# Eight modulation slabs as row products, fills moved to the start, chunk 3 converted early

## The reference, cut to what matters

```python
mod = silu(c) @ mod_w + mod_b                       # six vectors of 1024
sh1, sc1, g1, sh2, sc2, g2 = split(mod, 6)
h = rmsnorm(x, norm1_g) * (1 + sc1) + sh1
z = h @ w_in + b_in                                 # 1024 x 5646
x = x + g1 * mixer(z)                               # S5, mLSTM, forgetting attention, gates, w_out
h = rmsnorm(x, norm2_g) * (1 + sc2) + sh2
x = x + g2 * ((silu(h @ w1) * (h @ w3)) @ w2)       # hidden width 2816
out = rmsnorm(x, final_g)
```

## Time and profile before

| what | value |
|---|---|
| median of 3 runs | 886.14 us |
| runs | 880.66 to 889.43 us |
| the profiled execution | 881.7 us |
| its span, first to last instruction | 880.0 us |
| mean granted TensorE clock | 0.993 |
| TensorE matmul busy | 850.4 us (97%) |
| VectorE, ScalarE, GpSimd busy | 442.4, 324.9, 32.9 us |

### The profile page before, as it was taken

How to read it: one execution, slowest core, us unless ns; L and a number is a source line. 1 busy time by engine, 2 the same in 40 slices (tenths; PEclk the granted TensorE clock), 3 DMA queues, 4 the chain that set the end, 5 groups by cost and what they waited for, 6 DMA issues and landing times.

```text
span 880.0 us, 10526 instructions
## 1 busy us (share of the span) xinstructions
PE 850.4 (97%) x3936; PEld 682.3 (78%) x3936; DVE 442.4 (50%) x719; ACT 324.9 (37%) x477; POOL 32.9 (4%) x46
## 2 busy tenths in 40 slices
PE   3989999999999999999999999999999999999997
PEld 1568888877877777777888878888888888888886
DVE  4789978236779553333883373333333333322222
ACT  4454445442232443433333563333333332222221
POOL 1010000000000000000001110000000000000110
PEclk9899999999999999999999999999999999999999
DMA  8923322347884211215323323333333333333322
GB/s 302 292 68 89 89 75 74 92 153 233 283 282 150 67 53 48 67 30 167 89 80 120 95 64 99 99 97 95 95 95 95 95 95 90 90 107 90 96 77 96
DMA packets 149372, 100.67 MB, mean 114 GB/s; under 512 B 11072, under 2 KB 142552, under 8 KB 148312
## 3 DMA queue, kind: packets, MB, share of 16 engines
q1 hardware_dynamic: 146080, 100.10, 37.3%
q10 hardware_dynamic: 3256, 0.10, 0.2%
HBM read 97.03 MB, written 2.10 MB: 113 GB/s over the span
## 4 chain that ended last, share of the span: by engine, by line
PE 90%; DVE 4%; ACT 2%; issue 1%; DMA 1%; SPq 1%; POOL 0%; DVEq 0%; ACTq 0%
PE bank L1608 25%; PE bank L1610 25%; PE bank L1609 25%; PE bank L1625 2%; PE bank L1819 2%; PE bank L1749 1%; PE bank L1841 1%; PE bank L1769 1%; PE bank L1780 1%; DMA modA<-in_mod_w 1%; PE bank L1866 1%; PE bank L1832 1%; PE bank L1817 1%; DVE wlo L1115 1%; ACT whi L631 1%
## 5 line engine op out<-in xcount | busy, mean ns | idle before, releaser
L1608 PE MATMUL bank<-h_lo,whi 128*128 128x512 f32 x712 | 285.6, 401 | 4.8 <-DVE wlo L1115 2.6
L1610 PE MATMUL bank<-h_hi,wlo 128*128 128x512 f32 x712 | 278.2, 391 | 0.0
L1609 PE MATMUL bank<-h_hi,whi 128*128 128x512 f32 x712 | 277.9, 390 | 0.0
L1608 PEld LDWEIGHTS bank<-h_lo,whi 128*128 128x128 f32 x712 | 134.1, 188 | 34.7 <-issue 4.4
L1609 PEld LDWEIGHTS bank<-h_hi,whi 128*128 128x128 f32 x712 | 134.2, 189 | 28.8 <-issue 1.7
L1610 PEld LDWEIGHTS bank<-h_hi,wlo 128*128 128x128 f32 x712 | 134.1, 188 | 28.8
L1115 DVE TENSOR_TENSOR wlo<-raw,whi 128x1024 fp32r<-128x1024 f32 x61 | 74.5, 1223 | 103.3 <-ACT whi L631 103.3
L631 ACT ACTIVATE whi<-raw 128x1024 fp32r<-128x1024 f32 x61 | 64.3, 1055 | 156.4 <-PE bank L1610 115.8
L1610 PE MATMUL bank<-a_hi,wlo 128*128 128x512 f32 x176 | 68.5, 389 | 0.0
L1608 PE MATMUL bank<-a_lo,whi 128*128 128x512 f32 x176 | 68.5, 389 | 0.0
L1609 PE MATMUL bank<-a_hi,whi 128*128 128x512 f32 x176 | 68.5, 389 | 0.0
(11 more groups left out here) (326 smaller groups left out, 996.6 us busy)
## 6 DMA issues: line engine op xcount, KB each, us to landing
raw<-in_ffn_w SPq DMA_DIRECT2D x60, 512.0 KB, 3.8
raw<-in_w_in SPq DMA_DIRECT2D x44, 512.0 KB, 4.0
slab<-in_mod_w SPq DMA_DIRECT2D x32, 512.0 KB, 5.7
modA<-in_mod_w SPq DMA_DIRECT2D x4, 1024.0 KB, 11.0
modB<-in_mod_w SPq DMA_DIRECT2D x4, 1024.0 KB, 19.7
raw<-in_w_out SPq DMA_DIRECT2D x8, 512.0 KB, 3.7
raw<-in_ffn_w SPq DMA_DIRECT2D x8, 384.0 KB, 3.2
xtok<-in_x SPq DMA_DIRECT2D x4, 512.0 KB, 5.0
```

Source lines behind the costliest of these rows:

```text
L1608: mm(dst, w_h, m_l, start=first, stop=False)
L1609: mm(dst, w_h, m_h, start=False, stop=False)
L1610: return mm(dst, w_l, m_h, start=False, stop=last)
```

## The change

Five edits go together. (a) `keep_clock(12)` stands ahead of the first `mod_rows`, and `keep_clock(5)` behind the shift columns is gone. (b) `mod_rows` runs over all eight slabs, so the row copies wait for slab 7, and the eight one-column products for slab 7 are gone; each scale column is one closed product. (c) Chunk 3 gets a buffer of its own for `whi` (`whi_3`, in the place of `tab_c`, which moves to 115 KiB), and `hi(3)`, `lo(3)` stand right behind `hi(2)`, `lo(2)`. (d) The FFN starts with three chunks per tile k: ACT converts the third ahead of the `h_hi` tiles, DVE takes its `lo4` behind the first `h_lo`. (e) As that chunk fills bank 2, the 1/rms broadcast uses bank 3.

```diff
+        whi_3 = at("whi_3", [P, KB, P], F32R, 67)
-        tab_c = at("tab_c", [P, NS5, P], F32, 67)
+        tab_c = at("tab_c", [P, NS5, P], F32, 115)
...
+        def w_high(s):
+            return whi_3[:] if s == 3 else whi[:, s % 3]
...
-                if s >= 3:
+                if s >= 4:
                     act.wait_ge(w_mm, s - 2)
-                A(whi[:, s % 3], raw[:, s % 4], ACT.Copy).then_inc(w_hi, 1)
+                A(w_high(s), raw[:, s % 4], ACT.Copy).then_inc(w_hi, 1)
...
             hi(2)
+            hi(3)
             for t in range(1, S_F1):
-                if t >= 3:
+                if t >= 4:
                     hi(t)
...
+            act.wait_ge(w_loaded[(S_F1 + 2) % 4], SLOT_LOADS[S_F1 + 2])
+            A(whi4[:, (S_F1 + 2) % 4], raw[:, (S_F1 + 2) % 4], ACT.Copy).then_inc(w_hi, 1)
             for k in range(KB):
...
-            for s in range(S_F1 + 2, S_F1 + 4):
-                act.wait_ge(w_loaded[s % 4], SLOT_LOADS[s])
-                act.wait_ge(w_mm, S_F1)
-                A(whi4[:, s % 4], raw[:, s % 4], ACT.Copy).then_inc(w_hi, 1)
+            s = S_F1 + 3
+            act.wait_ge(w_loaded[s % 4], SLOT_LOADS[s])
+            act.wait_ge(w_mm, S_F1)
+            A(whi4[:, s % 4], raw[:, s % 4], ACT.Copy).then_inc(w_hi, 1)
...
             lo(2)
+            lo(3)
...
-                if t >= 3:
+                if t >= 4:
                     lo(t)
...
-                V.tensor_tensor(htmp[:, k % 4], x1g[:, k], ps[2][:], ALU.mult).then_inc(s_h2, 1)
+                V.tensor_tensor(htmp[:, k % 4], x1g[:, k], ps[3][:], ALU.mult).then_inc(s_h2, 1)
                 if k and k - 1 not in H2_POOL:
                     h2_lo(k - 1)
+                if k == 1:
+                    lo4(S_F1 + 2)
             h2_lo(KB - 1)
-            lo4(S_F1 + 2)
             lo4(S_F1 + 3)
...
-                              start=(k == 0), stop=(k == KB - 2))
-                    if k == KB - 2:
+                              start=(k == 0), stop=(k == KB - 1))
+                    if k == KB - 1:
                         ins.then_inc(s_mrow, 1)
...
-                        mm(ps[7][:, KB + 4 * n + i:KB + 4 * n + i + 1], modrow[:, n, i * P:(i + 1) * P],
-                           ones[0:1, 0:1], start=(n == 0 and i == 0), stop=False)
-                pe.wait_ge(s_mod0[KB - 1], 16)
-                for i in range(KB):
-                    ins = mm(ps[7][:, KB + i:KB + i + 1], modB[:, 3, D + i * P:D + (i + 1) * P], cf[:, KB - 1:KB],
-                             start=False, stop=(i == KB - 1))
+                        ins = mm(ps[7][:, KB + 4 * n + i:KB + 4 * n + i + 1], modrow[:, n, i * P:(i + 1) * P],
+                                 ones[0:1, 0:1], start=True, stop=True)
                 ins.then_inc(s_mod1, 1)
...
-            for k in range(KB - 1):
+            keep_clock(12)
+            for k in range(KB):
                 mod_rows(k)
...
             mod_scale_columns()
             mod_shift_columns()
-            keep_clock(5)
...
-                for w in range(2):
+                for w in range(3):
                     s = S_F1 + w
+                    if k == 0 and w == 2:
+                        pe.wait_ge(w_lo, s + 1)
                     ins = split_mm(ps[w][:], whi4[:, s % 4, k], wlo[:, s % 4, k], h_hi[:, k], h_lo[:, k],
                                    k == 0, k == KB - 1)
                     if k == KB - 1:
                         ins.then_inc(w_mm, 1)
```

More of the change, by code:

```diff
@@ L1114, in lo @@
                 dve.wait_ge(w_hi, s + 1)
-                V.tensor_tensor(wlo[:, s % 4], raw[:, s % 4], whi[:, s % 3].bitcast(F32),
+                V.tensor_tensor(wlo[:, s % 4], raw[:, s % 4], w_high(s).bitcast(F32),
                                 ALU.subtract).then_inc(w_lo, 1)
@@ L1936, in _ @@
                 for k in range(KB):
-                    ins = split_mm(ps[s % 2][:], whi[:, s % 3, k], wlo[:, s % 4, k], h_hi[:, k], h_lo[:, k],
+                    ins = split_mm(ps[s % 2][:], w_high(s)[:, k], wlo[:, s % 4, k], h_hi[:, k], h_lo[:, k],
                                    k == 0, k == KB - 1)
@@ L2009, in _ @@
             for t in range(NT):
-                ins = mm(ps[2][:, t * P:(t + 1) * P], rstd[:, t:t + 1].broadcast_to([P, P]), ident[:],
+                ins = mm(ps[3][:, t * P:(t + 1) * P], rstd[:, t:t + 1].broadcast_to([P, P]), ident[:],
                          start=True, stop=True)
@@ L2025, in _ @@
                         ins.then_inc(w_mm, 1)
[L2026 to L2032, removed]
+            s = S_F1 + 3
+            pe.wait_ge(w_lo, s + 1)
+            for k in range(KB):
+                ins = split_mm(ps[3][:], whi4[:, s % 4, k], wlo[:, s % 4, k], h_hi[:, k], h_lo[:, k],
+                               k == 0, k == KB - 1)
+            ins.then_inc(w_mm, 1)
             with pe.Fori(0, NF // 2 - 1) as i:
```

## The result

The changed kernel took 878.96 us in the median of 22 executions (876.37 to 886.08), the kernel before 886.18 us (880.02 to 889.43) beside it. The ratio is 0.9945, 95% interval 0.9925 to 0.9965: faster by 0.55% (4.9 us), clear of noise and under 1%. The sum forecast 2.2 us and 883.9; the time lies inside the range, but more was won than the sum says. Two later comparisons gave 0.9956 (0.9927 to 0.9985) and 0.9964 (0.9938 to 0.9990). All 46 executions of the changed kernel have a mean of 880.0 us, 105 of the kernel before 883.7: **3.7 us**, good to about 1 us. The 105 are those of the three later sets; with the 22 beside the first result (mean 885.3) it is 883.9, and the difference 4.0.

What follows compares the result with a forecast made beforehand. TensorE holds 90% of the chain, so only its waits, late feeding or half clock count. `modc` 1.9 us earlier plus 0.3 slack gives 2.2 us, FFN 0: from the median 886.14 to 883.9 us, range 879.0 to 888.4.

Steps and rivals of the forecast that it cites:

- Part 1: Modulation rows at the start: twelve early fills and eight slabs as rows bring `modc` 1.9 us earlier, at 39.85.
- the 0.75 us I gave them: Modulation rows: gain remaining from the early fills after ACT's copies hold the transposes, carried through slabs 4 to 7.
- Part 2: Behind the shift columns: without fills PE starts chunk 0 near 42.0; the half-clock loss lies inside the `wlo` 4 wait.
- Part 3: Chunk 3 converted early: its 2.63 us wait goes, but chunk 4 waits 1.1 to 2.8 us for `wlo` 4, starting at 69.3.
- the 0.3 of the sum: Ahead of chunk 4: slack that `wlo` 4 had, added to 1.9 us for the 2.2 us gain at the start.
- Part 4: FFN start: 0.4 us removed, 0.35 added, fifth chunk's `wlo` without cover; taken as 0.
- A: Front counts in full, `wlo` 4 no bound: 3.7 to 5.2 us by chunk 4, 880.9 us; chance 0.07.
- B: Start: clock not kept, as transposes don't count as busy, or fills late; `modc` at 41.5, 885.6 us; chance 0.25.
- C: FFN: fifth chunk's load lands late behind the new order, 0.8 us lost, 884.7 us; chance 0.13.
- D: Chunks 0 and 1 stay at half clock without fills ahead; low until 60 gives 888.1 us; chance 0.08.

Runs made afterwards that it cites:

- wlo4_first: Changed kernel with VectorE's order changed: `wlo` 4, 5 ahead of the b_blocks, `wlo` 6 ahead of the last four angle groups; ratio to before 0.9949, mean 879.0 us.
- fills_back: Changed kernel with the five fills behind the shift columns again; ratio to before 0.9974, mean 879.6 us.
- wlo4_again: Same kernel as wlo4_first, run again beside the changed kernel; ratio to before 0.9938, mean 878.1 us.
- ffn_only: Kernel before with only parts (d) and (e), three chunks per tile at the FFN start; ratio to before 1.0018, mean 885.4 us.
- wlo4_fills_back: wlo4_first's kernel with the five fills behind the shift columns again; ratio to before 0.9927, mean 878.1 us.
- start_only: Kernel before with only parts (a) and (b), the row edits and moved fills; ratio to before 0.9973, mean 881.6 us.
- chunk3_only: Kernel before with only part (c), the early conversion of chunk 3; ratio to before 0.9984, mean 882.3 us.

## Why the prediction was right, and where its sum was short

- **Part 1, `modc` 1.9 us earlier.** Measured: 2.2 in two of three traces of the changed kernel (39.54 for 41.75), set by VectorE's `wlo` 0 and 1, as written; 43.01 in the other. Over all ten traces with eight slabs as rows `modc` lies at 40.1 in the mean, over the four with the old columns at 42.05: 2.0 us. But the part of the fills in it was wrong: the 0.75 us I gave them are not there. Rows of slab 4 begin at 28.5 to 28.9 in seven of the eight traces with the fills and, without, at 28.6 or 29.2. What moved `modc` is the shift columns. They took 1.95 us in seven of ten traces with eight slabs as rows (2.03, 2.52 and 3.17 in the rest), 3.55 or more in all four with the old columns, and they ended 2.3 us sooner, though the last 512-column products ended 1.2 us later. Part of this is the order: in wlo4_first, where the clock fell at 38.02 as before, the columns took 3.17 us, and `modc` still came at 40.75. The rest is the clock, which fell at 36 to 38 us there and at 38 to 42 here, once not at all. That the longer rows keep the clock up is a guess; no run changed that alone.
- **Part 2.** Right: PE starts at 41.7 at half clock, and the loss vanishes in the wait for `wlo` 4. The 1.4 us of the old fills were there in the trace of before (in fills_back they were 0.4) and worth nothing.
- **Part 3, the step that was short.** "DVE has no idle between `wlo` 2 and 69.91 + 1.22 = 71.13, and the edit only moves 1.2 us within that stretch." A busy row is not all work: 1.12 us of it was a tensor_scalar held by a memset. Moving `wlo` 3 into the memset's time freed that. The slack of `wlo` 4 was also a little more than the 0.3 of the sum: 0.50 us between its end and chunk 4 before, 0.05 after. With `modc` that makes 2.2 + 0.45 + 1.1 = 3.75, against 3.8 at chunk 4.
- **Part 4.** Right: 0 forecast, 0.1 measured.
- **Rivals.** A fell: chunk 4 waits. B happened in the first of three traces, with x late as well, but not by the transposes on which the prediction put it. There and in wlo4_again (fall at 15.8) the clock fell inside slab 0's rows, behind 2.42 and 2.25 us in which PE was idle; in the other six traces with the twelve fills PE was idle there for 0.2 to 1.8 us, and the clock held through the transposes. In wlo4_again it cost nothing: `modc` came at 39.62. C did not happen, by a margin of 0.14 us. D fell: the low stretch behind the columns was 6.8 us, as before.
- **How far the rows explain the time.** The 3.8 us hold between two single traces, and the traced execution of before is a slow one for its clock: it lies 1.0 us above its kernel's own line, those of the changed kernel 0.1 and 0.4 below theirs and, in the first trace, 0.6 above. At equal low time the two kernels differ by 2.5 to 2.9 us, which is nearer to the 2.2 of the sum; about 1 us more of the 3.7 in the means goes with 2.2 us less of low time. Whether the change brings that or chance does stays open. The 7.2 us between the medians of the first set are more than any step explains. That the time fell into the range says little: the range is 9.4 us wide.
- The prediction held that a change under 1% can't be told from none. The interval here was 0.2% to either side, and 0.55% was clear of it.

## What to carry to other kernels

Before an engine's stretch is called incompressible, its rows' durations should be held against like rows elsewhere: a 128x8 operation of 1.34 us beside siblings of 0.17 us names a conflict, and the other engine's rows at that time name the partner. A wait that is removed should be followed to the next instruction that the same feeding engine owes; here that told where the wait would go, and reordering that engine's list took it away. Fills that keep the clock are worth only what the work behind them can use; either set here could go without a loss that 12 executions show. A pair of traces can say where time goes and still overstate how much: against the many executions of both kernels, 3.8 us became 2.7 at equal low time and 3.7 in the means.

## What the hardware showed that I had not expected

- The memset of GpSimd that writes 128x3072 held a tensor_scalar of VectorE for 1.12 us and left tensor_tensors alone (0.28 us beside it and apart). The held row is shown as busy, not as idle, and ends where the memset ends (55.11 and 55.08).
- The spread of this kernel is mostly clock: executions at 0.995 mean clock took 876.5 us (ten of 46), at 0.987 883.1 (ten). By the slope of 0.43 a low stretch of 3.4 us costs about 1.5 us, an estimate.
- Waits of PE of 1.96 to 2.23 us ahead of chunk 3, 4 or 7 went with a fall of the clock in four traces: it came between 0.1 us before the end of the wait and 1.1 us behind it (at 67.0 in ffn_only, 67.6 in fills_back, 72.4 in the first trace of the changed kernel, 85.1 in wlo4_fills_back). Others of 2.04, 2.33 and 2.63 us, in start_only, chunk3_only and before, were not followed by one.
